# Four attention heads in one step, mLSTM sample work in strips of the array, and the head and column loops written out

## The reference

```
z = rmsnorm(x) @ w_in            # mLSTM q,k,v,out-gate,i/f-gates | attention q,k,v | two merge gates
A = mLSTM(4 heads of 256, chunks of 128 tokens) -> norm -> sigmoid gate -> @ w_proj_a
    per chunk: S = (q k^T) * D;  num = S v + sc * (q C);  den likewise with n
               C' = wc * C + (k * ws)^T v;   n' likewise
    the 8 sample sequences have a C, n, m each, given as inputs and returned
B = attention over a window of 128 (16 heads of 64, 4 of keys and values), a sink per head -> @ w_proj_b
    m = max(max s, sink);  p = exp(s - m);  probs = p / (sum p + exp(sink - m));  o = probs v
x = x + (sigmoid(g_a) * A + sigmoid(g_b) * B) @ w_out
x = x + MoE(rmsnorm(x))          # 32 experts, two per token
```

## Time and profile before

| | |
|---|---|
| three runs | 2077.96, 2082.3 (median), 2087.96 us |
| the profiled execution | 2088.7 us, span of its instructions 2087.0 us |
| PE busy / DVE / ACT / POOL | 1807.8 / 910.8 / 705.6 / 439.1 us |
| four heads | 50.08 to 669.45 us |
| column chunks | 669.45 to 840.67 us |
| attention blocks | 840.67 to 1196.80 us |
| sample attention, projections, MoE, output | 1196.80 to 2087.0 us |

### The profile page before, as it was taken

The page is one execution under the profiler, slowest core; times in us unless marked ns, Lnnn a source line. Parts: engine busy times, 40 slices in busy tenths (PEclk is TensorE's granted clock), DMA queues, the critical chain, the costliest instruction groups (busy, mean ns, idle before and its releaser), DMA issues.

```text
span 2087.0 us, 29582 instructions
## 1 busy us (share of the span) xinstructions
PE 1807.8 (87%) x11381; PEld 1608.7 (77%) x11382; DVE 910.8 (44%) x1710; ACT 705.6 (34%) x1271; POOL 439.1 (21%) x241
## 2 busy tenths in 40 slices
PE   5999899999999799999999957999897388988880
PEld 4888898897998799887778747999897376777760
DVE  5422222222222001445555544243424478788966
ACT  4322122222122122333333323221213166667752
POOL 3001101101002000000000022000004278888752
PEclk9999999999999999999999958999999699999995
DMA  5033502503504423152222144344114188889956
GB/s 169 13 90 77 113 21 76 113 21 82 108 21 89 96 81 112 46 169 93 71 67 76 64 149 156 97 124 155 54 71 154 55 289 310 315 320 333 325 185 253
DMA packets 147568, 272.10 MB, mean 130 GB/s; under 512 B 44124, under 2 KB 114076, under 8 KB 134060
## 3 DMA queue, kind: packets, MB, share of 16 engines
q1 hardware_dynamic: 111792, 210.68, 30.7%
q0 software_dynamic: 16736, 40.14, 7.2%
q10 hardware_dynamic: 18912, 19.47, 3.1%
HBM read 223.14 MB, written 65.38 MB: 138 GB/s over the span
## 4 chain that ended last, share of the span: by engine, by line
PE 66%; DVE 12%; ACT 7%; issue 7%; DMA 3%; DVEq 3%; SPq 1%; another core or an unknown queue 1%; POOL 1%; POOLq 0%; ACTq 0%
PE pb L769 13%; PE pb L770 13%; PE pb L771 13%; PE pb L960 4%; DVE dl L2232 3%; ACT Pm L1411 2%; PE pw L769 2%; PE pw L876 2%; PE pw L770 2%; PE pw L771 2%; ACT dh L1264 2%; DVEq L2239 1%; PE pq L849 1%; PE pw L865 1%; PE pq L993 1%
## 5 line engine op out<-in xcount | busy, mean ns | idle before, releaser
L769 PE MATMUL pb<-whi,aTl 128*128 128x256 f32 (+1 forms) x1296 | 378.1, 292 | 22.0 <-ACT zo L1264 13.1
L770 PE MATMUL pb<-wlo,aTh 128*128 128x256 f32 (+1 forms) x1296 | 368.0, 284 | 0.0
L771 PE MATMUL pb<-whi,aTh 128*128 128x256 f32 (+1 forms) x1296 | 366.1, 283 | 0.0
L769 PEld LDWEIGHTS pb<-whi,aTl 128*128 128x128 f32 (+1 forms) x1296 | 235.3, 182 | 37.9 <-issue 21.0
L769 PE MATMUL pb<-aTh,wlo 128*128 128x352 f32 x720 | 239.0, 332 | 27.5 <-issue 14.5
L771 PEld LDWEIGHTS pb<-whi,aTh 128*128 128x128 f32 (+1 forms) x1296 | 236.2, 182 | 1.0
L770 PEld LDWEIGHTS pb<-wlo,aTh 128*128 128x128 f32 (+1 forms) x1296 | 235.0, 181 | 2.0
L771 PE MATMUL pb<-aTh,whi 128*128 128x352 f32 x720 | 235.8, 328 | 0.0
L770 PE MATMUL pb<-aTl,whi 128*128 128x352 f32 x720 | 235.8, 327 | 0.0
L1635 DVE TENSOR_TENSOR wlo<-stage,whi 128x2048 fp32r<-128x2048 f32 x34 | 77.7, 2286 | 225.0 <-ACT whi L1264 224.7
L769 PEld LDWEIGHTS pb<-aTh,wlo 128*128 128x128 f32 x720 | 139.3, 193 | 26.7 <-issue 23.7
(11 more groups left out here) (397 smaller groups left out, 3617.6 us busy)
## 6 DMA issues: line engine op xcount, KB each, us to landing
stage<-in_w_in SPq DMA_DIRECT2D x30, 1024.0 KB, 5.8
raw<-in_w_gate_e SPq DMA_DIRECT2D x19, 1024.0 KB, 7.0
raw<-in_w_up_e SPq DMA_DIRECT2D x19, 1024.0 KB, 7.9
raw<-in_w_down_e SPq DMA_DIRECT2D x19, 1024.0 KB, 7.3
stage<-in_w_gate_e SPq DMA_DIRECT2D x13, 1024.0 KB, 5.8
stage<-in_w_up_e SPq DMA_DIRECT2D x13, 1024.0 KB, 8.7
stage<-in_w_down_e SPq DMA_DIRECT2D x13, 1024.0 KB, 7.6
zt_scratch<-zo ACTq DMA_DIRECT2D x80, 128.0 KB, 1.7
```

The source lines that it names most:

```text
L769: pe.matmul(out, ll, rh, start=first, stop=False)
L770: pe.matmul(out, lh, rl, start=False, stop=False)
L771: return pe.matmul(out, lh, rh, start=False, stop=last)
```

## The change

*Loops.* The loops over heads and over column chunks are written out on all engines, and the `If`s with them. `zo` has six buffers instead of two.

*Chunk.* The running maximum is kept as three bf16 parts (`nm3`, 68 rows of which 12 are used), so L828 becomes one bf16 product. DVE makes the parts in head 0, inside `gate_columns`; SP's loads of the states now wait for `h_set`, which comes after that.

*Sample tokens in strips.* Four sequences stand side by side: q C of chunk 8 goes to four groups of 32 output columns, and `t1`, `v1` and `kwb` hold 128 rows (four copies or parts of 32); a product with `fold` adds the four parts, one with `spread` makes the four copies of v. The state update takes one half of four sequences' states per step, from four groups of 32 rows into four banks, in four steps (j = 10 to 13) instead of eight.

*Attention.* A step takes four heads; there are four steps per block. The division is done by DVE on the probabilities in place, and the turn is a plain transpose. `against_v` runs after every step, that of step 3 inside the next block.

```diff
-            zo = [a1(f"zo{i}", [128, CW]) for i in range(2)]
+            zo = [a1(f"zo{i}", [128, CW]) for i in range(6)]
...
-            with sp.Fori(0, MH) as h:
+            for h in range(MH):
...
-                sp.wait_ge(gq_c, NT)
+                sp.wait_ge(h_set, 1)
                 sp.wait_ge(st_s, h * (10 * 16) + 16)
...
-                pe.matmul(b[0:n, 128:128 + n], ones4[:, 0:n], nmh[:, tok(c)], start=True, stop=False)
+                pe.matmul(b[0:n, 128:128 + n], ones3[:, 0:n], nmh[:, tok(c)], start=True, stop=False)
...
-                    for b in range(NB):
+                    for u in range(2):
                         for d in range(2):
-                            mm = pe.matmul(qc, qTm[:, d, b, :], sC[:, b, d, :],
-                                           start=(b == 0 and d == 0), stop=(b == NB - 1 and d == 1))
+                            for j in range(4):
+                                mm = pe.matmul(pq[32 * j:32 * j + 32, 1, 0:MD + 1], qTm[:, d, 4 * u + j, :],
+                                               sC[:, 4 * u + j, d, :],
+                                               start=(u == 0 and d == 0), stop=(u == 1 and d == 1))
...
+                    pe.wait_ge(m_t1, M(h, c))
+                    mm = pe.matmul(pq[0:n, 0, 0:MD + 1], C("fold"), t1[:, :], start=False, stop=True)
...
+            def spread_v(h):
+                pe.wait_ge(z_ev, h * 30 + (G_M + 12 + 9))
+                pe.wait_ge(m_st, M(h, NPT - 1))
+                pe.wait_ge(m_kw, K(h, NPT - 1))
+                pe.matmul(AB[1][:, 0:MD + 1], C("spread", TS), v1[0:TS, NT - 1, :], start=True, stop=True
+                          ).then_inc(v_sp, 1)
...
-                pe.wait_ge(u_sc, K(h, b - 1))
-                for d in range(2):
-                    mm = pe.matmul(pw[:, d, 0:MD + 1], kwb[:, b, d * 128:(d + 1) * 128], v1[0:TS, NT - 1, :],
+                for j in range(4):
+                    g = slice(32 * j, 32 * j + 32)
+                    mm = pe.matmul(SB4[j][:, 0:MD + 1], kwb[g, u, d * 128:(d + 1) * 128], v1[g, NT - 1, :],
                                    start=True, stop=True)
...
-                for e in range(2):
-                    for half in range(2):
-                        mm = pe.matmul(AB[u % 2][:, (2 * e + half) * 128:(2 * e + half + 1) * 128],
-                                       Pm[u % 2][:, e, half * 128:(half + 1) * 128], dg[u % 2][:, e, :],
-                                       start=True, stop=True)
+                for v in range(2):
+                    for e in range(2):
+                        for half in range(2):
+                            mm = pe.transpose(AB[v][:, (2 * e + half) * 128:(2 * e + half + 1) * 128],
+                                              Sm[p % 2][:, 2 * e + v, half * 128:(half + 1) * 128], ident)
...
+            def block_end(n):
+                against_v(n, 3)
+                pe.wait_ge(z_mm, G_G + 6 * n + 6)
+                pe.sem_inc(w_use, 1)
...
-                filler(n, 0, 12)
+                filler(n, 0, 14)
+                if n:
+                    block_end(n - 1)
...
-                for u in range(10):
-                    if u < 8:
-                        scores(n, u)
-                    filler(n, 30 + 12 * u, 42 + 12 * u)
-                    if 1 <= u <= 8:
-                        probs_t(n, u - 1)
-                    if u in (5, 9):
-                        against_v(n, u // 4 - 1)
...
+                for p in range(4):
+                    scores(n, p)
+                    filler(n, 30 + 26 * p, 56 + 26 * p)
+                    if p >= 1:
+                        probs_t(n, p - 1)
+                    if p >= 2:
+                        against_v(n, p - 2)
+                filler(n, 134, FILL)
+                probs_t(n, 3)
+                against_v(n, 2)
+            block_end(NPT - 1)
...
+                for k in range(3):
+                    part = nmb if k < 2 else nm3[64:64 + MH, :]
+                    ve.tensor_copy(part[:, :], nmrow[:, :])
+                    ve.drain()
+                    if k < 2:
+                        ve.tensor_copy(nm3[32 * k:32 * k + MH, :], nmb[:, :])
+                        ve.tensor_tensor(nmrow[:, :], nmrow[:, :], nmb[:, :], ALU.subtract)
+                        ve.drain()
...
-                for e in range(2):
-                    h = 8 * gp + 4 * e + j
-                    i_ = ve.tensor_scalar(dg[u % 2][:, e, :], C("ident"), rden[:, h:h + 1], None, ALU.mult)
-                i_.then_inc(a_d, 1)
...
+                x = Sm[p % 2][:, :, :].rearrange("p (e v) k -> p e v k", e=2)
+                ve.tensor_tensor(x, x, quad(rden, p).unsqueeze(3).to_broadcast([128, 2, 2, 256]), ALU.mult
+                                 ).then_inc(a_d, 1)
...
+                for p in range(4):
+                    masked_max(n, p)
+                    if p >= 1:
+                        probs_copy(n, p - 1)
+                    if p >= 2:
+                        split_lo_part(N_G + n + 1, 1 - n % 2, 2 * p - 4)
+                    divide(n, p)
+                    if p >= 2:
+                        split_lo_part(N_G + n + 1, 1 - n % 2, 2 * p - 3)
+                    if p == 1 and n + 1 < NPT:
+                        rotate_block(n + 1)
+                probs_copy(n, 3)
```

More of the change, by code:

```diff
@@ L354, in build @@
         z_ev = sem("z_ev")
-        z_st = [sem(f"z_st{i}") for i in range(2)]
+        z_st = [sem(f"z_st{i}") for i in range(len(zo))]
         gw_h = sem("gw_h")
@@ L601, in _ @@
             sp.wait_ge(st_m, 32)
[L602 to L603 removed]
+            for k in range(NZO):
+                sp.wait_ge(z_st[k], Z_D[k] + 16 * Z_STEP)
             sp.dma_start(sinks[:, :], attn_sinks.to_broadcast([128, AH])).then_inc(ld_a, 16)
@@ L901, in used @@
                 pe.sem_inc(w_use, 1)
-            with pe.Fori(0, MH) as h:
+            for h in range(MH):
                 for j in range(12):
@@ L928, in _ @@
                         pe.wait_ge(z_ev, h * 30 + (G_M + 12 + j))
-                        s2(h, j - 1)
+                        against_c(h, j - 1)
+                        against_v1(h, j - 1)
+                        new_state(h, j - 1)
                     if j == 9:
-                        s2(h, 8)
-                    if j >= 10:
-                        s3(h, j - 10)
-            with pe.Fori(0, 3) as i:
+                        against_c(h, 8)
+                        spread_v(h)
+                    if j == 10:
+                        against_v1(h, 8)
+                    if 10 <= j < 14:
+                        sample_states(h, j - 10)
+            for i in range(3):
                 for j in range(18):
@@ L1343, in square @@
                                accum_out=pst[0:n, 0, c:c + 1]).then_inc(hp_a, 1)
-            with act.Fori(0, MH) as h:
+            for h in range(MH):
                 split_hi(h * 4 + 1, 1, 1, lds(1, h, 4))
@@ L1909, in rotate_block, with probs_copy @@
+            def probs_copy(n, p):
+                ve.wait_ge(a_pt, AP_(n, p))
+                if AP_(n, p) > 2:
+                    ve.wait_ge(a_pv, AP_(n, p - 2))
+                for v in range(2):
+                    i_ = ve.tensor_copy(PTs[p % 2][:, :, v, :], AB[v][:, :].rearrange("p (k t) -> p k t", k=4))
+                i_.then_inc(a_pc, 1)
             def rotate_block(n):
@@ L1949, in _ @@
             rope(Xs, TS, cst[0:TS, co:co + 8], cst[0:TS, sn_:sn_ + 8]).then_inc(b_v, 1)
+            for i in range(2):
+                ve.wait_ge(st_o[i], 16 * (NPT + 1))
             ve.wait_ge(b_tr, 3)
@@ L2326, in _ @@
                 gp.dma_start(s_m[0].rearrange("b h -> h b"), mout[:, 1:1 + NB]).then_inc(st_m, 16)
-            with gp.Fori(0, MH) as h:
+            for h in range(MH):
                 gp.wait_ge(m_ce, K(h, NPT - 1))
@@ L2491, in constants @@
     put("bmq", np.broadcast_to((t // DS == np.arange(NB)[:, None])[None], (128, NB, TS)).astype(np.float32))
-    put("bmk", (i // DS == np.arange(NB)[None, :]).astype(np.float32))
+    put("bmk", (i % TS // DS == 4 * np.arange(2)[None, :] + i // 32).astype(np.float32))
+    put("sel3", ((i % 32 == np.arange(MH)[None, :]) & (i < 96)).astype(np.float32))
+    put("fold", (i % TS == np.arange(TS)[None, :]).astype(np.float32))
+    put("spread", (s == j % TS).astype(np.float32))
     sm = np.full((AG, 4, 2, DS, NB // 2, SMW), BIG, np.float32)
```

332 lines of the change are left out of this document (172 added, 160 removed).

## The result

The changed kernel takes 1957.9 us (median of four runs, 1952.3 to 1971.3), against 2081.6 for the kernel before: 0.941 of it, 95% interval 0.936 to 0.947. Forecast were 1967 and a range of 1938 to 2008. The profiled execution took 1960.2 us (span 1958.4). Later the same kernel was run again beside other experiments (label changed_again): 1959.9 us, 0.942 (0.939 to 0.945), with a profiled execution of 1963.0 us.

The account below looks back on a forecast made before the run. PE was taken to bound heads, column chunks and attention. From the profiled 2088.7 us, 65 for heads and chunks, 50 for attention and 6.4 for the slow profiled execution came off: 1967 us, range 1938 to 2008.

Parts of the forecast that it names:

- attention: Attention stage: PE's work plus about 1 us wait makes 38.1 us a block, 306 us in all, a gain of 50.
- the column store: Heads: POOL's normaliser-column store, issued some 9 us earlier against the head's end, eases the 4.4 us wait; gain 4 us.
- `zo`: Column chunks: six buffers shorten the 11.5 us wait, of which 5 to 8 can stay; gain 6 us (0 to 13).
- the loops: Starts of three heads: waits and the slower products behind them go with the jump back; gain 14 us.
- maximum in bf16: Chunks: replacing L828 by a bf16 product saves 0.33 us each, 10.6 us in all (6 to 13).
- q C in strips: Sample tokens: q C falls from 7.14 to 2.2 us per head, 19.7 us saved in all (0 to 21).
- state update: Heads: four steps at 0.75 us instead of eight at 1.13, 6.0 us saved per head, 24 in all.
- head 0: Head 0: seven added DVE rows delay set-up, state loads and the weight load behind; loss 8.8 us (6 to 12).
- rival (d): Attention: transposes lower PE's clock for the fillers behind them, costing 64 us, 2031 us in all; chance 0.04.
- (b): Attention: DVE sets the step, 9.3 us instead of 7.3, so the gain of 50 goes, 2017 us; chance 0.07.
- Rival (c): Heads: the column store still stops instructions, gains of 4 and 6 go, each head waits 4.4 + 2.0; 1990 us; chance 0.13.
- The last step: Whole kernel: 6.4 us taken off the sum because the profiled execution was that far above the median of three runs.

Follow-up runs that it names:

- splits_ahead: Changed kernel with both strips of the weight's rest made ahead of the probabilities' copy in attention steps 2 and 3: 1953.9 us, 0.937 of the kernel before.
- no_max: Kernel before without L828, the product that adds the running maximum: 2065.0 us in one run, beside a median of 2086.4 for the kernel before.
- zo_two: Changed kernel with two `zo` buffers instead of six: 1994.0 us, 0.956 of the kernel before.
- loops_alone: Kernel before with only the loops over heads and column chunks, and the branches in them, written out: 2053.6 us, 0.985 of the kernel before.
- all_four: Changed kernel with early maximum parts, fourth weight load ahead of state loads, normaliser column stored as rows, splitting strips ahead of the copy: 1922.5 us, 0.924 of the kernel before.
- rows_store: Changed kernel with the normaliser column turned by PE transposes and stored as eight 1 KB rows, not 4-byte elements: 1950.9 us, 0.936 of the kernel before.

## Why the prediction was right, and where it was not

The time, the mechanisms of the three largest terms and attention came out; the terms for the column store and `zo` were wrong in kind, and that the sum came out is in part luck: they cancelled against two that were too small, the maximum and the loops. PE's first product of the heads stands at 50.40 in the trace before, not at 50.08, which is two products of the gates too early; the table goes by that.

| term | forecast | measured | from |
|---|---|---|---|
| maximum in bf16 | 10.6 | 14.7 | period 6.27 to 5.81, 8 chunks, 4 heads |
| q C in strips | 19.7 | 20.8 | 7.07 to 1.87, 4 heads |
| state update | 24 | 23.5 | 8 x 1.06 to 4 x 0.65, 4 heads |
| token groups with nothing behind them | 0 | 3 | 2.86 instead of 3.07, four per head |
| `spread`, `fold` | -4.2 | -4.7 | 0.62 + 0.55, 4 heads |
| head 0 | -8.8 | -8.4 | start of s1 of chunk 2, 7.5 later from the stage's start, and 2 x 0.46 gained till then |
| loops, column store and `zo` together | 24 | 18 to 22 | rest of 67.3 (first trace) and 71.6 (second) |
| heads and column chunks | 65 | 67 to 72 | |
| attention | 50 | 50.3 | 356.13 to 305.86 |
| what the change doesn't touch | 6.4 | 11 and 4.3 | last two stretches 12.3 and 4.9 shorter, heads begin 1.3 and 0.6 later |

*Right.* PE sets the time of all three stages, so that each product's length came out of it. The pace of the strips, estimated from the sample attention's rows, was 2.2 us and measured 1.87; that is 3.8 times less than 7.07. The Trainium skill ("TensorE: Matmul & The Clock Gate", Part 3, measured speedup) gives 3.07 times for four row strips, by which I had 2.3, and 2.38 for three column strips. For four column strips the measurement here decides. Attention's stage was forecast at 306 us and is 305.9, with one wait per block ahead of the last transposes and for the division, as said; splits_ahead shows its cause. Of its gain 38.2 us are PE's busy time and 12.1 its idle time; the parts of the attention change were not run one by one. The clock is 1.00 there, so rival (d) is out, and a block of 38.3 us puts (b) out.

*The maximum* was mis-sized. The step "a record's busy time overlaps the next, so I take 0.33" read only the product's own row: the period fell by 0.46, as the new product takes 0.06 and 0.10 more stood in the row ahead of the old one (no_max). The ninth chunk, left out of the forecast, gives next to nothing: with 32 columns the old product took 0.08 us.

*The column store* is the step that failed. "That store is now issued some 9 us earlier against the head's end ... I count 4 us of gain" has the sign wrong. Earlier means ahead of the head's last stores of `zo`, and these queue behind it. zo_two shows the price with the old two buffers, 9.3 to 11.5 us at the ends of heads 0 to 2; the new buffers pay for that, and in the column chunks, where I looked for their 6 us, they brought 1 to 3 (171.2 to 168.2 and 170.3). Set against the 23.7 us of loops_alone, which hold the unsettled 6.4, store and buffers together cost 1 to 6 us, where 10 of gain were forecast. I had taken two parts of the change apart that hold one another up. Rival (c) named the right store, but for the waits that have a name the wrong victim: not instructions, but ACT, which stands in the start of its own transfer. Its sum is off as well: three waits of 6.4 us are 19, not 13, which makes 1996.

*Loops.* Forecast were 14 us for the three head starts, and they make 15. I put the wait at 230.42 down to the column store. It is gone in loops_alone, which stores at the same place, but one trace does not settle it, since no_max has the loops and only 1.56 us there; what this wait is for stays open.

*The last step*, 6.4 us off because the profiled execution was above the median, was an allowance without a cause. One possible cause is in the last section.

## What to carry to other kernels

Before an edit makes something finish earlier, look at what is queued behind it on the DMA queues, not on its engine alone: here the earlier store would have cost 30 to 36 us, had the same change not brought buffers. A store of single elements is worth a transpose. When products go to separate groups of the array, deal them out in turn.

## What was not expected of the hardware

MoE's 32 experts run in one of two rhythms, and the same kernel shows both. PE's first products of the second matrix, in the first trace and then in changed_again's:

```profile
1558.99 0.50 PE L784 MATMUL pq<-dh,hTl 128*128 128x512 f32 x1 [1.44 <-DVE hTl L2325]
...
1570.23 0.47 PE L784 MATMUL pq<-dh,hTl 128*128 128x512 f32 x1 [1.41 <-DVE hTl L2325]
...
1581.42 0.47 PE L784 MATMUL pq<-dh,hTl 128*128 128x512 f32 x1 [1.42 <-DVE hTl L2325]
...
1592.62 0.48 PE L784 MATMUL pq<-dh,hTl 128*128 128x512 f32 x1 [1.41 <-DVE hTl L2325]
```

```profile
1553.73 0.79 PE L784 MATMUL pq<-dh,hTl 128*128 128x512 f32 x1 [2.74 <-DVE hTl L2325]
...
1565.13 0.47 PE L784 MATMUL pq<-dh,hTl 128*128 128x512 f32 x1
...
1577.36 0.59 PE L784 MATMUL pq<-dh,hTl 128*128 128x512 f32 x1 [2.45 <-DVE hTl L2325]
...
1588.77 0.47 PE L784 MATMUL pq<-dh,hTl 128*128 128x512 f32 x1
```

An expert takes 11.19 us, or 11.41 and 12.23 in turn for the first 14; the stage is 420.0 or 428.0 us long. The kernel before had the second rhythm in its trace (428.7), loops_alone the first, all_four the second. So 8 us of any comparison of two single executions of this kernel can be this alone. What sets the rhythm wasn't tried, but in seven traces it goes with TensorE's clock at the start. In the four with the longer rhythm (the kernel before, no_max, changed_again, all_four) the second expert's first 24 products run at a granted clock of 1.00, the upper of its two levels, in 5.7 us; PE then waits 2.7 us for DVE's `hTl`, and the products behind the wait start at 0.50. In the three with the shorter one (the first trace, loops_alone, rows_store) the 24 products take 7.0 us at a mean of 0.79; PE waits 1.4 us and goes on at 1.00. In all seven the first product on `hTl` starts 9.76 us behind the first of the 24, so a faster PE gains nothing there. What sets the clock of the 24 products, no run shows.
